# Attention mixers of the later block in another order, with a changed opening, post-norm and dense entry

## What is computed

```
for l in range(2):                       # second_block
    h = h + 0.5 * rmsnorm(swiglu(rmsnorm(h)))
    u = rmsnorm(h, mix_pre_g[l])
    qa,ka,va, qb,kb,vb, qc,kc,vc, gl = split(u @ w_in[l])   # 3 x 512, 512+128+128, 3 x 512, 3 x 1024
    oa = neighbourhood_attention(qa, ka, va, rpb)            # 8 heads of 64, bias by position
    ob = sliding_window_attention(rope(qb), rope(kb), vb, sink)  # 8 heads, 2 of keys and values
    oc = differential_attention(rope(qc), rope(kc), vc, lam)
         # 4 heads: softmax(q0 k0) - lam * softmax(q1 k1), times v; then rmsnorm of each head
    merged = sum(sigmoid(gl + b_gate) * (branches @ w_branch))   # 3 branches
    h = h + rmsnorm(merged @ w_out[l])
    h = h + 0.5 * rmsnorm(swiglu(rmsnorm(h)))
```

## Time and profile before

| | |
|---|---|
| median of 3 executions | 2783.58 us (2783.43 to 2784.21) |
| the profiled execution's own time | 2782.96 us |
| its span on the core, first to last instruction | 2781.2 us |
| PE / DVE / ACT / POOL busy | 92% / 65% / 50% / 7% of the span |
| mean granted TensorE clock | 0.960 of full speed |
| the mixer stages, later block, layer 0 | na 95.8, sw 77.8, diff 101.9 us |
| the same, layer 1 | na 95.8, sw 77.8, diff 101.9 us |

### The profile page before, as it was taken

One profiled execution on the slowest core, in us unless ns is written; L12 is line 12 of the kernel. 1 busy time (PEld: TensorE's weight loads), 2 busy tenths in 40 slices (PEclk: granted clock), 3 DMA queues, 4 the chain that ended last, 5 costly groups with the idle time before them and its releaser, 6 DMA issues. The chain is left out here.

```text
span 2781.2 us, 32412 instructions
## 1 busy us (share of the span) xinstructions
PE 2564.1 (92%) x11950; PEld 2103.3 (76%) x11950; DVE 1798.0 (65%) x1716; ACT 1398.5 (50%) x1485; POOL 193.8 (7%) x270
## 2 busy tenths in 40 slices
PE   7899998699999999999799879889999998888998
PEld 5678776588888888888688767668878876766786
...
GB/s 233 123 189 186 176 149 92 107 344 361 347 351 339 366 349 345 360 355 354 195 236 197 111 133 129 115 167 212 181 166 241 199 129 137 122 122 142 205 188 61
DMA packets 88119, 592.12 MB, mean 213 GB/s; under 512 B 11288, under 2 KB 11472, under 8 KB 20304
## 3 DMA queue, kind: packets, MB, share of 16 engines
...
...
## 5 line engine op out<-in xcount | busy, mean ns | idle before, releaser
L566 PE MATMUL pp<-hi_a,uT_hi 128*128 128x512 f32 x2224 | 901.3, 405 | 48.0 <-DVE uT_lo L1733 22.1
L568 PE MATMUL pp<-hi_a,uT_lo 128*128 128x512 f32 x2224 | 877.4, 395 | 0.0
L567 PE MATMUL pp<-lo_a,uT_hi 128*128 128x512 f32 x2224 | 877.3, 394 | 0.0
L1814 DVE TENSOR_TENSOR lo_a<-raw_a,hi_a 128x2048 fp32r<-128x2048 f32 x282 | 652.9, 2316 | 126.5 <-ACT hi_a L1297 126.5
L1297 ACT ACTIVATE hi_a<-raw_a 128x2048 fp32r<-128x2048 f32 x282 | 537.8, 1908 | 6.4 <-DMA raw_a<-in_moe_gu 5.9
L566 PEld LDWEIGHTS pp<-hi_a,uT_hi 128*128 128x128 f32 x2224 | 427.2, 192 | 138.0 <-issue 27.8
L568 PEld LDWEIGHTS pp<-hi_a,uT_lo 128*128 128x128 f32 x2224 | 426.0, 192 | 92.3
L567 PEld LDWEIGHTS pp<-lo_a,uT_hi 128*128 128x128 f32 x2224 | 428.0, 192 | 82.4
L567 PE MATMUL acc<-lo_b,hT_hi 128*128 128x512 f32 x792 | 311.9, 394 | 0.0
L1847 DVE TENSOR_TENSOR lo_b<-raw_b,hi_b 128x2048 fp32r<-128x2048 f32 x116 | 265.9, 2292 | 46.4 <-ACT hi_b L1315 45.3
L566 PE MATMUL acc<-hi_b,hT_hi 128*128 128x512 f32 x576 | 227.8, 395 | 10.8 <-DVE lo_b L1847 10.8
...
## 6 DMA issues: line engine op xcount, KB each, us to landing
...
```

What stands on the lines that cost most here:

```text
L566: nc.tensor.matmul(out_ap, l_hi, r_hi, start=start, stop=False, skip_group_check=True)
L567: nc.tensor.matmul(out_ap, l_hi, r_lo, start=False, stop=False, skip_group_check=True)
L568: return nc.tensor.matmul(out_ap, l_lo, r_hi, start=False, stop=stop, skip_group_check=True)
L1814: ins = nc.vector.tensor_tensor(lo_a[:, slot, cs], raw_a[:, slot, cs], hi_a[:, slot, cs].bitcast(F32), ALU.subtract)
```

## The change

**Tables.** In `MIX` the value chunk va changes places with qk1. `UNITS`, `SPLIT` (now also with the number of units of the item that come before the split) and `ROTATE` are new: splits of na in items 1, 2, 4, 6, 7 (before 0, 1, 2, 4, 6), of sw in 0, 2, 4, 6, 7 (before 0, 1, 3, 5, 7); rotations in na items 4 and 5 (before 5 and 6) and sw items 1 and 3 (before 2 and 4).

**Within a head.** ACT and DVE do an item's split and rotation before most of its units. The units between come before scores of head 0 on DVE. `lo_turned` and `hi_turned` come before `combine` and before the next exponential.

**Maps of diff.** The scaling instruction L2002 is gone: the scale goes into the eviction of qc (`factor_of`), row maxima and exponential read the scores in PSUM, and so q by k of a later head waits for the exponential and not for DVE, and the exponential for the combination before.

**End of the mixer.** The norms of all four heads are taken behind the last output, and units and transposes are in another order.

**Elsewhere.** `post_norm` is in two parts, the first of which doesn't need the root, with the add in the second. In the dense feed-forward, the transposes of the first chunk stand between the two token tiles of the second. At the opening x comes as two tiles, the first weight chunk in halves and PE starts on its first half, with the transposes of token tile 1 among the first chunk's units (`first_mixer`, not shown); ACT runs an exponential first, and the earlier block's two opening chunks are split by halves.

The diff, cut to its core:

```
@@ -66,7 +66,7 @@
...
-MIX = (("in", "qk0", 512, 0), ("in", "qk1", 512, 512), ("in", "va", 512, 1024), ("in", "kb", 256, 1536),
+MIX = (("in", "qk0", 512, 0), ("in", "va", 512, 1024), ("in", "qk1", 512, 512), ("in", "kb", 256, 1536),
...
@@ -76,11 +76,13 @@
...
-UNITS = {"na": (1, 1, 1, ((3, 2), (2, 0), (2, 0), (2, 0), (2, 0), (2, 0), (2, 0), (2, 0))),
-         "sw": (1, 1, 1, ((1, 1),) * 8), "diff": (1, 1, 2, ((2, 1), (2, 2), (2, 1), (2, 1)))}
-
-SPLIT = {"na": (0, 1, 2, 4, 6), "sw": (0, 1, 3, 5, 7), "diff": (0, 1, 2, 3)}
-ROTATE = {"na": {5: "kb", 6: "qb"}, "sw": {2: "qc", 4: "kc"}, "diff": {}}
+UNITS = {"na": (1, 1, 1, ((2, 1), (2, 0), (2, 1), (2, 0), (2, 1), (2, 0), (2, 0), (2, 0))),
+         "sw": (1, 1, 2, ((0, 1),) + ((1, 1),) * 7), "diff": (1, 1, 2, ((2, 1), (2, 2), (2, 1), (2, 0)))}
+
...
+         "diff": {0: 0, 1: 0, 2: 2, 3: 1}}
+ROTATE = {"na": {4: "kb", 5: "qb"}, "sw": {1: "qc", 3: "kc"}, "diff": {}}

...
@@ -449,8 +458,12 @@
...
+            sp.dma_start(x[:, 0, :], a["x"][0, 0:P, :]).then_inc(s_xin[0], 16)
+            sp.dma_start(raw_a[:, 0, 0:2048], a["w_in"][0][:, 0:2048]).then_inc(s_early, 16)
+            sp.dma_start(x[:, 1, :], a["x"][0, P:2 * P, :]).then_inc(s_xin[1], 16)
+            sp.dma_start(raw_a[:, 0, 2048:4096], a["w_in"][0][:, 2048:4096]).then_inc(s_al[0], 16)
...
@@ -684,15 +697,18 @@
...
-                        pe.wait_ge(s_ppv, c.half * 4 + (2 * c.rest + ppv0))
+                        pe.wait_ge(s_ppv, c.half * 4 + (2 * c.rest - opening + ppv0))
...
                     for tt in range(tiles):
+                        if opening and tt == 1:
+                            turn(Chunk(c.half, c.rest - 1))
...
@@ -823,7 +840,9 @@
...
-                    if M >= 2:
+                    if kind == "diff" and m >= 2:
+                        pe.wait_ge(s_exp, n["exp"] + m - 1)
+                    elif M >= 2:
                         pe.wait_ge(s_sc, M - 1)
...
@@ -996,16 +1015,18 @@
...
-                units(1)
+                units(2)
                 for tt in range(TT):
                     n["rows"] += 1
                     pe.wait_ge(s_rows, n["rows"])
                     turn(mixb, OUT_AT["diff"], tt)
-                units(4)
+                    if tt == 0:
+                        units(1)
+                units(3)
...
@@ -1377,8 +1403,11 @@
...
+                if kind == "diff" and m >= 2:
+                    act.wait_ge(s_comb, n["comb"] + m // 2)
                 for tt in range(TT):
-                    last = nc.scalar.activation(sc[:, M % 2, tt, :], sc[:, M % 2, tt, :], ACT.Exp,
+                    src = acc[:, M % 2, tt * S:(tt + 1) * S] if kind == "diff" else sc[:, M % 2, tt, :]
+                    last = nc.scalar.activation(sc[:, M % 2, tt, :], src, ACT.Exp,
...
@@ -1432,6 +1461,8 @@
...
                         copy_pT(it)
+                    if turned and it < TT:
+                        turned(it)
...
@@ -1482,46 +1515,34 @@
...
                     def item(it, part):
-                        if part == 0:
-                            beside(it)
-                        units(UNITS[kind][3][it][part])
+                        todo = UNITS[kind][3][it][part]
                         if part == 0 and it in SPLIT[kind]:
+                            units(SPLIT[kind][it])
+                            todo -= SPLIT[kind][it]
                             split()
+                        if part == 0 and gates and it == gates[0]:
+                            for tt in range(TT):
+                                gate(gates[1], tt)
+                        units(todo)
...
+                units(2)
                 for tt in range(TT):
                     hi_turned(tt)
                     act.sem_inc(s_mixed, 1)
-                units(1)
-                gate(2, 1)
+                    gate(2, tt)
+                    if tt == 0:
+                        units(1)
...
@@ -1952,32 +1980,39 @@
...
+                n["ss"] += 1
+                dve.wait_ge(s_ss, n["ss"])
+                link(nc.vector.tensor_tensor(merged[:, tt, :].rearrange("p (h c) -> p h c", h=2),
+                                             acc[:, 2 * tt:2 * tt + 2, :],
+                                             vec[:, slot, :].rearrange("p (h c) -> p h c", h=2), ALU.mult))
...
+            def post_back(tt):

                 wait_rstd()
-                o = merged[:, tt, :]
-                link(nc.vector.scalar_tensor_tensor(out=o.rearrange("p (h c) -> p h c", h=2),
-                                                    in0=acc[:, 2 * tt:2 * tt + 2, :], scalar=rstd[:, tt:tt + 1],
-                                                    in1=vec[:, slot, :].rearrange("p (h c) -> p h c", h=2),
-                                                    op0=ALU.mult, op1=ALU.mult))
-                link(nc.vector.tensor_tensor(x[:, tt, :], x[:, tt, :], o, ALU.add))
+                link(nc.vector.scalar_tensor_tensor(out=x[:, tt, :], in0=merged[:, tt, :], scalar=rstd[:, tt:tt + 1],
+                                                    in1=x[:, tt, :], op0=ALU.mult, op1=ALU.add))
...
@@ -1999,11 +2034,11 @@
...
-                        ins = nc.vector.tensor_scalar(s_o_, s_in, SCALE, None, ALU.mult)
...
+                        nc.vector.tensor_reduce(negmax[:, M % 4, :], s_in, AX_X, ALU.max, negate=True).then_inc(s_nm, 1)
+                        signal(s_sc)
...
@@ -2076,6 +2111,8 @@
...
+                if opening:
+                    opening()
                 for m in range(per):
                     scores(m)
...
@@ -2087,6 +2124,9 @@
...
+                    if early and it < TT:
+                        early(it)
+                    if it + 1 < items:
                         if kind == "diff":
                             combine(it + 1)
...
@@ -2271,8 +2311,8 @@
...
+                            nc.vector.tensor_scalar(dst[:, 1, c0:c0 + width], pp[:, 1, 0:width],
+                                                    factor_of(which)[:, 1:2], None, ALU.mult).then_inc(s_fev, 1)
...
                     def item(it):
-                        if kind != "na" and it < TT:
-                            lo_turned(it)
-                        if beside:
-                            beside(it)
-                        units(UNITS[kind][3][it][0])
+                        todo = sum(UNITS[kind][3][it])
                         if it in SPLIT[kind]:
-                            split()
-                        units(UNITS[kind][3][it][1])
+                            units(SPLIT[kind][it])
+                            todo -= SPLIT[kind][it]
+                            if kind == "diff" and it == 3:
+                                lo_half(0)
+                            else:
+                                split()
                         if it in ROTATE[kind]:
                             turn(ROTATE[kind][it])
                             if ROTATE[kind][it] in ("qb", "kc"):
                                 signal(s_rope)
+                        units(todo)
...
+                    attend(kind, dst, ahead, item, done, lambda: units(UNITS[kind][1]), turned)
...
-                units(1)
+                mix("diff", mixb[:, :, 1280:1792], turned=lo_turned, done=head_squares)
+                wait_rstd()
+                gains["heads"] = gain()
+                for tt in range(TT):
+                    for h in range(3):
+                        head_norm(tt, h)
                 wait_rstd()
                 for tt in range(TT):
                     head_norm(tt, 3)
                     signal(s_rows)
-                for tt in range(TT):
-                    lo_turned(tt)
+                lo_half(1)
+                units(2)
+                lo_turned(0)
                 units(1)
...
+                lo_turned(1)
                 units(1)
                 lo_half(0)
                 units(1)
                 lo_half(1)
-                units(1)
                 lo_tile(0)
-                units(1)
+                units(2)
                 lo_tile(1)
```

139 lines of the change are left out of this document (74 added, 65 removed).

## The result

| | before | changed |
|---|---|---|
| median | 2783.51 us (4 runs, 2781.55 to 2784.21) | 2689.07 us (4 runs, 2683.53 to 2692.20) |
| ratio, 95% interval | | 0.966 (0.964 to 0.9679) |
| profiled execution / its span | 2782.96 / 2781.2 | 2692.02 / 2690.2 |
| mean granted clock | 0.960 | 0.970 |

The kernel before, run again beside each group of them, had medians of 2782.0 to 2782.7. The runs of the changed kernel differ more than those of before; why is the first finding.

A forecast was written before the change was run, and what follows sets the result against it. PE, busy 92% of the span, was taken as the bound, losing only waits and low clock. Two mixers 66, opening 1.5, post-norm 5.3 and dense entry 5.0 sum to 77.8 off 2782.96: forecast 2706 us, range 2690 to 2740.

The forecast's parts named there:

- na, 15.7 saved: Neighbourhood attention, each mixer: idle 16.65 becomes 5.8, and of four low clock stretches one stays; 15.7 us saved.
- sw, 3.6 lost: Sliding window attention, each mixer: waits on pair copies raise idle from 6.50 to 8.55, plus one low stretch; 3.6 us lost.
- diff, 23.0 saved: Diff attention, each mixer: idle falls by 16.6 and four low clock stretches go, 6.4; 23.0 us saved.
- hidden by PE already: In diff, DVE loses eight scalings of 0.69, 5.5 us, said to pay only through the new order.
- each of them can turn into a quarter: I take off 2: Some eight places in a mixer where PE nearly waits: 2 us deducted, 35.1 counted as 33 per mixer.
- Post-norm, 5.3: Post-norms: the wait of 0.88 goes five times (4.4) and 0.9 at the very end; 5.3 us saved.
- Dense entry, 5.0: Dense feed-forward entries: waits of 1.21 and four of 1.08 go, 5.5; taken as 5.0 us, down to 2.
- Opening, 1.5: Kernel start: PE starts some 5 earlier but first scores need POOL's bias; 1.5 us saved, between -1 and 2.1.
- B: the pairs take over: Five pair copies per mixer behind splits in na and sw, at 3.10 + 1.6 each; 2734 us, chance 0.20.
- The clock (D): Rival: sw's row of short waits keeps PE's clock at the lower level; 2848 us, chance 0.04.
- The maps in PSUM: Diff's maxima and exponential reading PSUM: same price as before, bounds under 2 us a mixer; the added wait priced at nothing.
- case C: Rival, better than laid: na's waits of 3.8 and 2.0 and the low stretch don't come; 2691 us, chance 0.13.

The follow-up runs named there:

- na_old: Changed kernel with the neighbourhood attention (na) in the order of before: qk1 before va, old units, splits and rotations; 2724.43 us, 32.4 slower.
- second trace: Trace of the changed kernel measured again, unchanged; that measurement gave 2692.44 us (2687.51 to 2694.64).
- sw_old: Changed kernel with the tables of before in the sliding window attention (sw) only; 2685.79 us, 6.2 faster by the median, ranges overlapping.
- diff_all_old: Changed kernel with four edits of diff (maps, units between, turned halves, six norms) and the mixer's end order undone; 2741.36 us, 49.3 slower.
- postnorm_old: Changed kernel with the old form of the post-norm, both instructions behind the root; 2700.96 us, 9.0 slower.
- best1: Changed kernel with na's chunk 6 split in item 5, qb rotated in item 6, and sw's tables of before; 2675.13 us, 17 faster.
- maps_sbuf: Changed kernel with the maps of diff scaled and copied to SBUF by DVE again, maxima and exponential read there; 2697.28 us, 5.3 slower.

## Why the prediction missed by a little

The direction, the places and most of the terms were right; the sum was too small. Against the profiled executions 77.8 were forecast and 90.9 measured (2782.96 - 2692.02). By the spans (91.0) the mixer stages give 76.3 where 66 stood, all else 14.7 where 11.8 stood. So the steps that failed are, by size: the loss in sw, charged 5.2 too high for the two mixers; the deduction of 4 that no row called for; and the post-norm, whose clock was left out. Whether the median of a few runs fell just below 2690 or just above it was chance, 2689.1 in one measurement and 2692.4 in the other. The steps one by one:

- **na, 15.7 saved.** Right: 13.9 and 16.7. Both waits left were forecast (2.0 and 3.8; 1.74 and 3.05). `na_old` puts the gain on the tables.
- **sw, 3.6 lost.** A term mis-sized: 1.0 in the changed kernel's first trace, 1.9 and 2.6 in its second. The forecast idle was 8.55, the measured 6.3 (5.7 and 7.8 in the second), since the first pair waited 0.36 and not 0.8 and the last one 0.7 to 1.3 wherever the clock had been low before it; only where it stayed up did the forecast 2.7 come, 2.75. For two mixers the forecast was 5.2 short, against the second trace 2.6. That it is a loss, and lies in the pair copies, `sw_old` and the waits show.
- **diff, 23.0 saved.** Right, 23.8 in both, and shown by `diff_all_old`. The shares inside were not. The new reading of the maps was put at nothing, "hidden by PE already", and measures 5.3 us when taken back; the 4.30 was shared by two edits; the end's order, undone last, carries 8 of the 23. The trace of before has three low stretches here and three in na, of 3.4 to 10.2 us, and not four of 3.3; the loss of PE time is about the same, some 7 and 6.5. A sum of stage waits can be right where the credit given to each edit is not.
- **"each of them can turn into a quarter: I take off 2".** A step without a reason in the rows: a deduction by feeling of 4 us for two mixers. Nothing of it came; 35.1 stood and 38.1 was measured, mean of the two mixers' three stages.
- **Post-norm, 5.3.** Mis-sized: 9.0 by `postnorm_old`. The waits were right, 5.6. The failed step is that I counted low clock stretches only in na and diff and not for the 0.88 next to a wait of 2.33.
- **Dense entry, 5.0.** Mis-sized the other way, 3.2 by the waits, 3.8 by the median. I named the low half of the down weights as what is late next; in the trace it was the same hidden rows on DVE, which hold the PSUM that the second chunk needs: 0.69 behind each mixer, 0.97 in the earlier block.
- **Opening, 1.5.** Between -1 and 2.1 as said; the traces have 1.9 at the first head, the runs can't tell it.
- **"B: the pairs take over"**: its waits were there, 0.36 to 2.75, and all below its price of 3.10. **The clock (D)**: no; sw ran at 0.98 with 6.3 idle, and at 0.96 at the lowest in the second trace. But the reason given against it was too strong: the waits of 1.97 and 1.93 left the clock alone in before and in `best1`, while in `sw_old` it was low for 3.4 us behind the 1.98 and the 1.96 of either layer. The Trainium skill, page "TensorE: Matmul & The Clock Gate", section "A second HAM failure mode: psum-queue depth-cycling", tells of a kernel whose frequent short idle times make the clock swing. The traces agree in a small way: it fell behind 8 of 27 waits of 1.74 too.
- **The maps in PSUM.** The Trainium skill, page "VectorE: DVE Perf Modes", section "Rules for kernel authors", says to accept the slow rate of a PSUM source or to copy to SBUF first where many operations follow. It gives no number for many; the prediction took two readers for many, and here that is wrong: `maps_sbuf`, which copies, is 5.3 us slower.
- **The range.** Its low end, 2690, left out half of case C. The forecast took a low stretch as a fixed 1.6 for each wait above 2.3, without a spread; the nine runs of one program cover 11 us, with the clock, and that should have been added on both sides.

Outside the mixer stages the waits give 5.6 (post-norms), 3.2 (entries) and 2 to 3 (opening) of the 14.7. That the remaining 3 or so are clock fits the 1.6 us gained in the stretches ahead of na, whose idle time is unchanged, and is not tested by itself.
